# First differential head in another order on four engines, and one root ahead of one low split in the last delta pair

## What is computed

```python
def first_block(x, ...):                  # layer 0: MLA attention + conv FFN, layer 1: differential attention + conv FFN
    for i in range(2):
        a = rms_norm(h, norm_g[i, 0]);  a = mla_mixer(a, ...) if i == 0 else diff_mixer(a, ...)
        h = h + rms_norm(a, norm_g[i, 1])
        h = h + rms_norm(conv_ffn(rms_norm(h, norm_g[i, 2]), ...), norm_g[i, 3])

def diff_mixer(x, w_qkv, lam_p, subln_g, w_o, layer_idx):     # 8 heads, two score maps each
    q, k, v = split(x @ w_qkv)
    p = softmax(q k^T * scale - slope * |distance|)            # for both maps of a head
    a = p[:, :, 0] - lam * p[:, :, 1]
    o = rms_norm(a v, subln_g) * (1 - lam_init)
    return o @ w_o

def hybrid_layer(x, ...):                 # softmax attention and a gated delta rule side by side, both gated and added
    o_b = rmsnorm(gated_deltanet(q_b, k_b, v_b, g, beta), gdn_norm_w)   # 8 heads, here in 4 pairs
    merged = sigmoid(gate_a) * y_a + sigmoid(gate_b) * y_b
    return x + rmsnorm(merged @ w_out, post_norm_w)
```

## Time and profile before

| | us |
|---|---|
| median of three executions | 1066.64 |
| lowest and highest | 1065.28, 1067.12 |
| the profiled execution's own time | 1066.56 |
| its span, first to last instruction | 1064.8 |
| PE busy | 1036.0 (97%) |
| DVE, ACT, POOL busy | 663.6, 560.7, 417.6 |
| mean granted clock of TensorE | 0.997 of full speed |

### The profile page before, as it was taken

One profiled execution on the slowest core, in us unless ns is written; L12 is line 12 of the kernel. 1 busy time (PEld: TensorE's weight loads), 2 busy tenths in 40 slices (PEclk: granted clock), 3 DMA queues, 4 the chain that ended last, 5 costly groups with the idle time before them and its releaser, 6 DMA issues.

```text
span 1064.8 us, 21773 instructions
## 1 busy us (share of the span) xinstructions
PE 1036.0 (97%) x8216; PEld 950.1 (89%) x8216; DVE 663.6 (62%) x1074; ACT 560.7 (53%) x1022; POOL 417.6 (39%) x283
## 2 busy tenths in 40 slices
PE   9899999999999999999999999999999999999997
PEld 7799699999978998699999987899999899999996
DVE  4555767677665665776766755766676555554545
ACT  4555665555555555756555565644443355554433
POOL 1000234433351334334333463865653365534431
PEclk9999999999999999999999999999999999999999
DMA  8333465665543443365656434333213245546551
GB/s 317 120 124 128 132 218 186 195 197 178 177 159 130 140 147 131 114 225 183 205 184 201 159 102 148 110 120 109 92 61 120 80 133 149 155 137 209 199 181 43
DMA packets 46136, 162.27 MB, mean 152 GB/s; under 512 B 5248, under 2 KB 5504, under 8 KB 45952
## 3 DMA queue, kind: packets, MB, share of 16 engines
q1 hardware_dynamic: 44784, 156.78, 45.1%
q0 software_dynamic: 1296, 4.72, 1.4%
HBM read 160.43 MB, written 1.05 MB: 152 GB/s over the span
## 4 chain that ended last, share of the span: by engine, by line
PE 90%; DVE 3%; POOL 3%; ACT 2%; issue 1%; DMA 1%; DVEq 0%; SPq 0%; ACTq 0%
PE work L399 14%; PE work L401 14%; PE work L400 14%; PE work L1688 9%; PE acc L399 6%; PE acc L400 6%; PE acc L401 6%; PE work L2410 4%; PE work L2422 2%; PE acc L2422 2%; POOL low L368 1%; PE acc L1939 1%; PE acc L1953 1%; PE acc L1955 1%; POOL stat L559 1%
## 5 line engine op out<-in xcount | busy, mean ns | idle before, releaser
L368 POOL TENSOR_TENSOR low<-raw,high 128x1024 fp32r<-128x1024 f32 x109 | 265.7, 2441 | 293.4 <-ACT high L357 290.9
L368 DVE TENSOR_TENSOR low<-raw,high 128x1024 fp32r<-128x1024 f32 (+2 forms) x184 | 273.2, 1493 | 159.3 <-ACT high L357 159.2
L357 ACT ACTIVATE high<-raw 128x1024 fp32r<-128x1024 f32 (+2 forms) x293 | 299.5, 1032 | 43.9 <-DMA raw<-in_w_out 29.1
L399 PE MATMUL work<-xh,high 128*128 128x256 f32 (+1 forms) x1032 | 290.0, 281 | 0.7 <-DVE low L368 0.7
L400 PE MATMUL work<-xl,high 128*128 128x256 f32 (+1 forms) x1032 | 287.9, 279 | 0.0
L401 PE MATMUL work<-xh,low 128*128 128x256 f32 (+1 forms) x1032 | 287.8, 279 | 0.0
L399 PEld LDWEIGHTS work<-xh,high 128*128 128x128 f32 (+1 forms) x1032 | 193.2, 187 | 7.6 <-issue 4.8
L400 PEld LDWEIGHTS work<-xl,high 128*128 128x128 f32 (+1 forms) x1032 | 193.3, 187 | 2.0 <-issue 0.3
L401 PEld LDWEIGHTS work<-xh,low 128*128 128x128 f32 (+1 forms) x1032 | 193.3, 187 | 0.2
L1156 POOL TENSOR_TENSOR h<-gelu,cv 128x256 f32<-128x256 f32 x44 | 50.5, 1149 | 198.7 <-ACT gelu L1077 102.0
L1688 PE MATMUL work<-xh,high 128*128 128x256 f32 x256 | 76.7, 300 | 0.0
(11 more groups left out here) (385 smaller groups left out, 2201.2 us busy)
## 6 DMA issues: line engine op xcount, KB each, us to landing
raw<-in_w_ffn SPq DMA_DIRECT2D x132, 512.0 KB, 4.3
raw<-in_w_out SPq DMA_DIRECT2D x39, 512.0 KB, 4.5
raw<-in_w_att SPq DMA_DIRECT2D x32, 512.0 KB, 3.7
raw<-in_w_diff SPq DMA_DIRECT2D x31, 512.0 KB, 4.3
raw<-in_w_gdn SPq DMA_DIRECT2D x24, 512.0 KB, 4.0
raw<-in_w_mla SPq DMA_DIRECT2D x8, 512.0 KB, 3.6
raw<-in_w_gdnz SPq DMA_DIRECT2D x8, 512.0 KB, 3.6
raw<-in_w_mla SPq DMA_DIRECT2D x8, 384.0 KB, 3.1
```

Source lines behind the costliest of these rows:

```text
L357: act.activation(high[k][:, 0:w], raw[k][:, 0:w], ACT.Copy).then_inc(high_done[k], 1)
L368: eng.tensor_tensor(low[k][:, 0:w], raw[k][:, 0:w], high[k][:, 0:w], ALU.subtract).then_inc(low_done[k], 1)
L399: pe.matmul(out, lhs[0], rhs[0], start=start, stop=False)
```

## The change

In the differential phase head 0 gets an order of its own. On PE the scores of head 0 come right behind the projection of its values, then the turning of values 0, then queries and keys of head 1, and the projection of values 1 last, ahead of the turning of the probabilities. On ACT, behind the exponentials: high of queries 2, copy of q and k of head 1, copy of values 1, copy of the turned probabilities, high of values 2, high of keys 2. On DVE the copy of the turned values 0 and the low part of values 1 go behind the maxima of head 0, and low of queries 2 goes ahead of low of values 2. The lists of SP and POOL for this phase stay. In the last delta pair POOL makes the root of pair 2 ahead of the low part for slot 0. No instruction is added or taken away.

```diff
+        def first_head():
+            scores(0)
+            turn_values(0)
+            for k in range(2):
+                queries_keys(1, k)
+            values(1)
+            turn_prob(0, W[2])
+            turn_values(1)
+            pe.wait_ge(h["qkev"], 2 + DIFF_SEEN)
+            result(0)
...
         values(0)
-        turn_values(0)
-        head(0)
+        first_head()
         head(1)
...
         def head(i):                                  # diff_act
             first = isinstance(i, int) and i == 0
             exponentials(i)
-            if not first:
+            if first:
+                refill(split, ph["diff"], 0, 1)
+                take_qk(1)
+                take_values(1)
+                take_prob(0, W[2])
+                refill(split, ph["diff"], 2, 1)
+            else:
                 result_high(i - 1)
...
             refill(split, ph["diff"], 1, i + 1)
...
             maxima(i, chain)                          # diff_dve
+            if first:
+                take_values(0)
+                refill(split, ph["diff"], 2, 0)
             weights(i, chain)
             if not first:
                 result_low(i - 1)
-            refill(split, ph["diff"], 2, i + 1)
+                refill(split, ph["diff"], 2, i + 1)
             refill(split, ph["diff"], 0, i + 1)
+            if first:
+                refill(split, ph["diff"], 2, 1)
             refill(split, ph["diff"], 1, i + 1)
             take_values(i + 1)
...
-        take_values(0)
-        refill(split, ph["diff"], 2, 0)
         over(dve, HEADS - 2, head, 0)
...
+            result_root_pool(pool, i - 1)             # pair_pool, last pair
             refill(split, ph["att"], 0, 0)
-            result_root_pool(pool, i - 1)
             refill(split, ph["att"], 2, 0)
```

More of the change, by code:

```diff
@@ L1257, in result @@
             last.then_inc(h["pv"], 1)
+        def first_head():
[8 more added lines that the diff above has]
+            result(0)
         def head(i):
-            first = isinstance(i, int) and i == 0
-            if not first:
-                pe.wait_ge(h["ptev"], i + DIFF_SEEN)
+            pe.wait_ge(h["ptev"], i + DIFF_SEEN)
             scores(i)
             values(i + 1)
-            if not first:
-                turn_result(i - 1)
+            turn_result(i - 1)
             for k in range(2):
@@ L1269, in head @@
             turn_prob(i, W[2])
-            if not first:
-                add_output(i - 1)
+            add_output(i - 1)
             turn_values(i + 1)
@@ L1344, in head @@
             exponentials(i)
-            if not first:
-                result_high(i - 1)
-            take_values(i + 1)
-            refill(split, ph["diff"], 2, i + 1)
-            refill(split, ph["diff"], 0, i + 1)
-            take_qk(i + 1)
-            take_prob(i, W[2])
+            if first:
[5 more added lines that the diff above has]
+            else:
+                result_high(i - 1)
+                take_values(i + 1)
+                refill(split, ph["diff"], 2, i + 1)
+                refill(split, ph["diff"], 0, i + 1)
+                take_qk(i + 1)
+                take_prob(i, W[2])
             refill(split, ph["diff"], 1, i + 1)
```

## The result

The changed kernel takes 1068.49 us (median of ten executions) against 1066.32 for the kernel before: ratio 1.0021, 95% interval 1.0011 to 1.0030, so 2.2 us (1.2 to 3.2) slower. One of the ten executions took 2066.62 us and is left out of the ratio; the median of the other nine is 1068.36. Timed again beside the experiments it was 1068.55 against 1066.14, ratio 1.0023 (1.0014 to 1.0032). The forecast was 1067.9 with a range of 1065.8 to 1069.2. The profiled execution took 1067.77 us, 1.2 us more than that of before, with a span of 1065.9 against 1064.8; the median is 0.7 above it, and that gap is a part of the story.

A forecast was written before the change was run, and what follows sets the result against it. PE, busy for 97% of the span, was taken as the bound, so only its stops could be won. The root's -1.0 and head 0's +2.3 gave +1.3 on 1066.56, so 1067.9 us, range 1065.8 to 1069.2.

The forecast's parts named there:

- The root: Last delta pair: POOL's root ahead of the low split removes PE's wait before the turned result, -1.0 us.
- What PE would win: Head 0: without the early stops PE could start result 0 at 342.1, 2.2 us earlier than before.
- The order of loads: Head 0: queries 2 land at 342.9, PE stops 3 us before turning values 1, result 0 starts at 345.5.
- The step behind it: End of head 0: POOL's low part holds the mean; turned result at 351.8 to 352.05 against 349.59, part taken as +2.3.
- the waits of 0.45 and 1 us: PE in head 0: waits for low part of values 2 and for the turned result, covering up to 1.45 us.
- The sum: Whole kernel: -1.0 for the root plus +2.3 for head 0, +1.3 us.
- rival (b): TensorE's clock falls in head 0's new stop; mostly covered, 0 to +0.3 us; at full cost net +2.5, chance 0.15.
- the full price: Clock fall in head 0 costing +1.7 in full minus 0.45, net +2.5 us, 1069.1 us; chance 0.15.
- the landing of queries 2: Head 0: load of queries 2 issued at 338.1 lands 4.8 us later, at 342.9.
- an edge (5.7): Rival (c), head 0: load of queries 2 takes 5.7 instead of 4.8 us, +2.2 net, 1068.8 us; no separate chance given.

The follow-up runs named there:

- Exchanging the loads: Changed kernel with SP's three third-chunk loads in the order queries, values, keys instead of values, queries, keys: 1064.74 us, ratio 0.9988 to the kernel before.
- head 0 alone: Changed kernel with the root where it was, so only the new order of head 0: 1068.84 us, ratio 1.0026 to the kernel before.
- three idle products: Changed kernel plus three 128x512 products with unread results on PE in the new stop: 1066.69 us, ratio 1.0007 to the kernel before.
- ACT's high part later: Changed kernel with ACT's high part of queries 2 behind the copies of q and k, values 1 and turned probabilities: 1067.28 us, ratio 1.0008 to before.

## Why the prediction was right, and which term was too small

**The root (-1.0).** Right: -1.2 us alone, with an interval of -0.2 to -2.1. In the changed kernel it ran at 824.34 and not near 822, since everything there was 2.3 us later by then (DVE's mean at 824.09 instead of 821.79).

**What PE would win.** Right as far as it goes: the turned probabilities at 341.43 for a forecast 341.45.

**The order of loads.** Right: low part of values 1 done at 337.1 (337.4), load out at 337.85 (338.1), high part begun at 342.76 (342.9), turning of values 1 at 344.69 (344.95), result 0 at 345.23 (345.5). Exchanging the loads, and nothing else, took the whole cost away.

**The step behind it.** The mean was held as foreseen (1.60 us) and DVE's scaled result was ready at 351.52, so the forecast for PE, 351.8 to 352.05, met its 351.75. But PE came there by another way: at half clock it needed all the time from 345.23 for its own matmuls, and the waits of 0.45 and 1 us that I had drawn were filled by them. The sentence of the Trainium skill on the shared ports (page "SBUF — State Buffer", section "Who interferes with whom") agrees with the runs: the mean took 2.02 us beside POOL's low part and 0.17 without it.

**The sum was +1.3, the measured +2.2 and +2.4.** The interval of the first measurement (1.2 to 3.2) still holds +1.3, that of the second (1.5 to 3.4) just doesn't. So the sum was probably about 1 us too low, and two terms look mis-sized.

The first is rival (b). I held a fall of the clock likelier than not, priced it from one stretch of 3.4 us, and found it covered. That is what the first profile shows, and the profile of head 0 alone had one stretch too (0.66 from 345 to 350). I gave a second stretch behind the first too little weight: it is in one of the three profiles with the unfilled stop ahead of the turning of values 1, and costs 1.3 us at the turned result. Nor did I ask whether the fall at the boundary ahead of the delta phase recurs; it comes and goes, and costs 1.1. The executions spread accordingly: of the nineteen of the changed kernel, the four with a mean clock of 0.993 took 1069.32 to 1070.05 us, and the two shortest, 1066.34 and 1066.65, had 0.997 and 0.996. With the stop filled the median was 1.9 us lower. So 0.15 was probably too small a chance for the full price, though three profiles can't give its frequency. The rule of the page "TensorE: Matmul & The Clock Gate" of the Trainium skill, section "Why this matters for your kernels", to leave no long gaps between bursts of matmuls, bore on this change as the prediction said: the clock fell at each of the three stops, of 2.67, 3.00 and 3.28 us.

The second is the landing of queries 2. I took 4.8 us from one row. The first profile after had 4.8 too, but in five other profiles with the late load the same load took 5.1, 5.1, 5.2, 5.4 and 5.6 us, and what waits for it shifts with it. The prediction had this as an edge (5.7) and not as its middle. On the median this is about +0.4, from few samples.

Taken from its profile of one slow stretch in head 0 and a quick landing, the changed kernel is at +1.2 us, which is the forecast; that the two agree so closely is in part luck, since the second profile has one stretch more in head 0, one less at the boundary and a landing of 5.2. How the rest of the gap divides between clock and landing can't be told within the 1 us of these intervals: the kernel with three idle products lies at +0.55, and the two executions of head 0 alone with a clock of 0.999, less the 1.2 of the root, at +0.5 and +0.8, where the sum without any clock cost gives +1.3. So the sum for the work alone may even have been too high, and the clock's share larger than the gap; neither is shown.

## What to carry to other kernels

When work is reordered, follow the buffers that it frees to the queue that fills them: here a low part that no one on PE missed held a load, that load held another behind it on SP's queue, and an in-order engine stood at the second one in front of the copies that PE was waiting for. A stop of 2 to 3 us on TensorE costs more than its length when it lets the clock fall, and a profile shows one outcome of that; compare the times and the mean granted clock of all executions before you trust a single one. That mean also counts stretches in which TensorE has nothing to do; where a fall costs time is seen only in the windows of a profile.

## What the runs showed of the hardware that I had not expected

The granted clock fell behind the same stop for 3.4 us in one execution and for 6.8 us in another, with PE working through the second half. The fall at the last boundary ahead of the delta phase, too, was there in one profile and not in another of code that was the same up to there; it is worth about 1.1 us. In the profile with ACT's high part later it also fell between 450 and 460 us (0.92 and 0.74), where no other profile has a fall.

A product of 128x512 with float32 operands cost 0.86 us of PE's time, as two records of 0.59 us whose starts lie 0.43 apart; I had counted one.
